# Head sums of branch A as rounded part and remainder

## What is computed

```
y = moveaxis(y, 0, 1)                                  # (B, T, heads, 64)
mean = jnp.mean(y, -1, keepdims=True)
var = jnp.mean(jnp.square(y - mean), -1, keepdims=True)
y = ((y - mean) * lax.rsqrt(var + RWKV_LN_EPS)).reshape(B, T, BW) * ln_g + ln_b
bonus = jnp.sum(r * k * r_k.reshape(H, N), -1, keepdims=True) * v
return y + bonus.reshape(B, T, BW)
```

## Time and profile before

| | |
|---|---|
| median of three runs | 1074.45 us |
| the profiled execution | 1073.86 us |
| its span | 1072.0 us |
| TensorE busy in the span | 1048.0 us, 98% |
| VectorE busy | 586.9 us, 55% |
| GpSimd busy | 371.9 us, 35% |
| ScalarE busy | 315.5 us, 29% |
| mean granted TensorE clock | 0.998 |

### The profile page before, as it was taken

One profiled execution on the slowest core, in us unless ns is written; L12 is line 12 of the kernel. 1 busy time (PEld: TensorE's weight loads), 2 busy tenths in 40 slices (PEclk: granted clock), 3 DMA queues, 4 the chain that ended last, 5 costly groups with the idle time before them and its releaser, 6 DMA issues.

```text
span 1072.0 us, 22528 instructions
## 1 busy us (share of the span) xinstructions
PE 1048.0 (98%) x9816; PEld 824.5 (77%) x9816; DVE 586.9 (55%) x988; ACT 315.5 (29%) x508; POOL 371.9 (35%) x343
## 2 busy tenths in 40 slices
PE   7999999999999999999999999999999999999997
PEld 5686787777777877877877777877877778878885
DVE  3768943874463522622623139458888587433553
ACT  5545112421503203213211133335444330002221
POOL 1431543321466222122231223353334249662000
PEclk9999999999999999999999999999999999999999
DMA  9700111211111110111111121111111137302221
GB/s 355 276 19 12 47 52 47 72 30 35 40 28 36 40 37 27 40 37 36 31 37 31 37 62 30 50 51 36 42 36 42 36 104 260 108 25 98 101 77 59
DMA packets 80130, 70.24 MB, mean 66 GB/s; under 512 B 4128, under 2 KB 68896, under 8 KB 80032
## 3 DMA queue, kind: packets, MB, share of 16 engines
q1 hardware_dynamic: 74560, 49.34, 14.8%
q10 hardware_dynamic: 5472, 19.47, 5.1%
HBM read 64.59 MB, written 4.19 MB: 64 GB/s over the span
## 4 chain that ended last, share of the span: by engine, by line
PE 88%; DVE 6%; DMA 2%; SPq 2%; ACT 1%; issue 1%; ACTq 0%; DVEq 0%
PE bank L609 55%; PE bank L663 8%; PE bank L1144 8%; PE bank L715 2%; PE bank L1099 1%; DVE slots L1744 1%; DMA slots<-in_x 1%; PE bank L941 1%; PE bank L937 1%; PE bank L820 1%; DMA slots<-in_w_mod 1%; PE bank L888 1%; SPq L437 1%; DVE slots L1824 1%; PE bank L914 1%; DVE slots L1728 1%
## 5 line engine op out<-in xcount | busy, mean ns | idle before, releaser
L609 PE MATMUL bank<-hn_hi,w_hi 128*128 128x512 f32 x880 | 357.0, 406 | 2.3 <-DVE slots L1886 1.7
L609 PE MATMUL bank<-hn_hi,w_lo 128*128 128x512 f32 x880 | 343.4, 390 | 0.0
L609 PE MATMUL bank<-hn_lo,w_hi 128*128 128x512 f32 x880 | 343.0, 390 | 0.0
L523 POOL CAST w_hi<-w_raw 128x512 fp32r<-128x512 f32 x110 | 86.3, 784 | 535.0 <-PE bank L609 535.0
L609 PEld LDWEIGHTS bank<-hn_hi,w_hi 128*128 128x128 f32 x880 | 165.1, 188 | 42.4 <-issue 4.3
L609 PEld LDWEIGHTS bank<-hn_hi,w_lo 128*128 128x128 f32 x880 | 165.2, 188 | 36.1
L609 PEld LDWEIGHTS bank<-hn_lo,w_hi 128*128 128x128 f32 x880 | 165.3, 188 | 33.8 <-issue 1.9
L525 POOL TENSOR_TENSOR w_lo<-w_raw,w_hi 128x512 fp32r<-128x512 f32 x110 | 154.2, 1402 | 8.8
L1276 ACT ACTIVATE stage<-bank 128x512 f32<-128x512 f32 x64 | 38.1, 599 | 247.5 <-PE bank L609 232.4
L1255 ACT ACTIVATE slots<-bank 128x512 f32<-128x512 f32 x42 | 24.8, 599 | 123.0 <-PE bank L609 122.9
L1884 DVE TENSOR_TENSOR stage<-stage,bank 128x512 f32<-128x512 f32 x48 | 33.0, 687 | 40.4 <-PE bank L663 39.0
(11 more groups left out here) (334 smaller groups left out, 1547.8 us busy)
## 6 DMA issues: line engine op xcount, KB each, us to landing
w_raw<-in_w_in SPq DMA_DIRECT2D x110, 256.0 KB, 2.8
slots<-in_w_mod SPq DMA_DIRECT2D x16, 512.0 KB, 11.4
slots<-in_x SPq DMA_DIRECT2D x8, 512.0 KB, 9.2
w_branch<-in_w_branch SPq DMA_DIRECT2D x32, 128.0 KB, 2.9
slots<-in_w_mod ACTq DMA_DIRECT2D x8, 512.0 KB, 4.9
slots<-in_w_out ACTq DMA_DIRECT2D x8, 512.0 KB, 6.2
xr<-in_x ACTq DMA_DIRECT2D x8, 512.0 KB, 3.6
out<-xr ACTq DMA_DIRECT2D x8, 512.0 KB, 2.6
```

The source lines that it names most:

```text
L523: nc.gpsimd.tensor_copy(w_hi[p][:, :, :], w_raw[p][:, :, :]).then_inc(s_pool_step, 1)
L609: last = mm(o, w[p][:, k4, :], h[:, k, n * HALF:(n + 1) * HALF], start=(p == 0 and k4 == 0 and q == 0), stop=(p == 1 and k4 == 3 and q == 2))
```

## The change

A fp32 product per bank becomes two products of rounded operands, one with the input's rounded part and one with its remainder, added up in the bank; the stationary operand is `ones_r`, the table of ones copied once into a rounded tile. ScalarE makes the rounded parts by a copy and VectorE the remainders by a subtraction, for the mean (rounded part in slots 14 and 15, remainder in slots 6 and 7), for the variance (the same slots again, the remainder in place of the squares) and for the bonus (rounded part in slots 0 and 1, remainder in place in slots 8 and 9). The bonus input (L2058) is made earlier, ahead of the forget gate. The scan (L2065) waits for the variance group, as it writes slots 14 and 15.

```diff
--- before.py
+++ after.py
@@ -200,6 +200,8 @@
         s_a_sa_ready = sem("a_sa_ready")
         s_a_gnew_done = sem("a_gnew_done")
         s_a_mean_done = sem("a_mean_done")
+        s_sum_hi_ready = sem("sum_hi_ready")
+        s_sum_lo_ready = sem("sum_lo_ready")
         s_a_rk_ready = sem("a_rk_ready")
         s_a_bonus_done = sem("a_bonus_done")
         s_a_bonus_read = sem("a_bonus_read")
@@ -277,6 +279,7 @@
         lru_w_at = -(-nc.sbuf_base // 32) * 32
         lru_w = sb("lru_w", [P, 4, P])
         small = sb("small", [P, 80])
+        ones_r = sb("ones_r", [P, P], F32R)
         banks = ctx.enter_context(nc.psum_tensor("bank", [P, 8, HALF], F32))
         bank = [banks[:, i, :] for i in range(8)]
 
@@ -406,6 +409,9 @@
 
         y_lo = {s0: nc.alloc_sbuf_tensor_at(f"y_lo{s0}", [P, 2, T], F32R, offset=slots_at + row * s0)
                 for s0 in sorted(set(Y_SLOT.values()))}
+        sum_hi = [over(f"sum_hi{j}", slots_at + row * (14 + j), F32R) for j in range(2)]
+        bonus_hi = [over(f"bonus_hi{j}", slots_at + row * j, F32R) for j in range(2)]
+        bonus_lo = [over(f"bonus_lo{j}", slots_at + row * (8 + j), F32R) for j in range(2)]
         w_branch_lo = [nc.alloc_sbuf_tensor_at(f"w_branch_lo{i}", [P, 2, P], F32R, offset=w_branch_at + 8 * P * i)
                        for i in range(2)]
         w_branch_hi = [nc.alloc_sbuf_tensor_at(f"w_branch_hi{i}", [P, 2, P], F32R, offset=lru_w_at + 8 * P * i)
@@ -811,6 +817,10 @@
                 project_part(1 + j)
             project_part(3)
 
+            def sums_of(o, hi, lo, n):
+                mm(o[:, :], ones_r[:, :], hi[:, n * HALF:(n + 1) * HALF], start=True, stop=False)
+                return mm(o[:, :], ones_r[:, :], lo[:, n * HALF:(n + 1) * HALF], start=False, stop=True)
+
             def head_sums(src, turn):
 
 
@@ -1030,21 +1040,25 @@
             project(4)
             pe.wait_ge(s_a_y_ready, 16)
             pe.wait_ge(s_a_g_ready, 32)
+            pe.wait_ge(s_sum_hi_ready, 1)
 
             for j in range(2):
                 for n in range(2):
-                    mm(bank[4 + 2 * j + n][:, :], blockones, slot(4 + j)[:, n * HALF:(n + 1) * HALF],
-                       start=True, stop=True).then_inc(s_a_mean_done, 1)
+                    if n == 0:
+                        pe.wait_ge(s_sum_lo_ready, j + 1)
+                    sums_of(bank[4 + 2 * j + n], sum_hi[j], y_lo[6][:, j], n).then_inc(s_a_mean_done, 1)
             project(1)
-            head_sums(6, 2)
+            for j in range(2):
+                pe.wait_ge(s_sum_lo_ready, j + 5)
+                for n in range(2):
+                    sums_of(bank[4 + 2 * j + n], sum_hi[j], y_lo[6][:, j], n).then_inc(s_head_sums, 1)
             project_part(0)
             project_part(1)
             for j in range(2):
-                pe.wait_ge(s_a_rk_ready, j + 1)
+                pe.wait_ge(s_sum_lo_ready, j + 3)
                 for n in range(2):
                     pe.wait_ge(s_roots, 8 + 2 * j + n + 1)
-                    mm(bank[4 + 2 * j + n][:, :], blockones, slot(8 + j)[:, n * HALF:(n + 1) * HALF],
-                       start=True, stop=True).then_inc(s_a_bonus_done, 1)
+                    sums_of(bank[4 + 2 * j + n], bonus_hi[j], bonus_lo[j], n).then_inc(s_a_bonus_done, 1)
             turn_tile(BI)
             project_part(2)
             project_part(3)
@@ -1454,6 +1468,15 @@
 
             act.wait_ge(s_a_y_ready, 16)
             act.wait_ge(s_a_g_ready, 32)
+            nc.scalar.activation(ones_r[:, :], blockones, ACT.Copy).then_inc(s_sum_hi_ready, 1)
+            after(s_sum_hi_ready)
+            for j in range(2):
+                nc.scalar.activation(sum_hi[j], slot(4 + j), ACT.Copy).then_inc(s_sum_hi_ready, 1)
+                after(s_sum_hi_ready)
+            for j in range(2):
+                act.wait_ge(s_a_rk_ready, j + 1)
+                nc.scalar.activation(bonus_hi[j], slot(8 + j), ACT.Copy).then_inc(s_sum_hi_ready, 1)
+                after(s_sum_hi_ready)
             evac(2)
             for j in range(2):
                 nc.scalar.activation(b_f[j], b_f_raw[j], ACT.Sigmoid).then_inc(s_b_f_sig, 1)
@@ -1467,7 +1490,10 @@
             evac(2)
             act.wait_ge(s_a_centred, 4)
             squares(4, 6)
-            act.wait_ge(s_a_rk_ready, 2)
+            for j in range(2):
+                act.wait_ge(s_squares, 4 + j + 1)
+                nc.scalar.activation(sum_hi[j], slot(6 + j), ACT.Copy).then_inc(s_sum_hi_ready, 1)
+                after(s_sum_hi_ready)
             evac(1)
             roots(6, 2, 1.0 / 64, "ln_eps")
             act.wait_ge(s_b_d_ready, 1)
@@ -2040,6 +2066,22 @@
 
 
             for j in range(2):
+                dve.wait_ge(s_sum_hi_ready, j + 2)
+                dve.wait_ge(s_br_done, 32)
+                nc.vector.tensor_tensor(y_lo[6][:, j], slot(4 + j), sum_hi[j].bitcast(F32), SUB)\
+                    .then_inc(s_sum_lo_ready, 1)
+                dve.wait_ge(s_sum_lo_ready, after(s_sum_lo_ready))
+            for j in range(2):
+                nc.vector.scalar_tensor_tensor(out=slot(8 + j), in0=slot(8 + j), scalar=pc("rk", j),
+                                               in1=slot(10 + j), op0=MUL, op1=MUL).then_inc(s_a_rk_ready, 1)
+                dve.wait_ge(s_a_rk_ready, after(s_a_rk_ready))
+            for j in range(2):
+                dve.wait_ge(s_sum_hi_ready, j + 4)
+                nc.vector.tensor_tensor(bonus_lo[j], slot(8 + j), bonus_hi[j].bitcast(F32), SUB)\
+                    .then_inc(s_sum_lo_ready, 1)
+                dve.wait_ge(s_sum_lo_ready, after(s_sum_lo_ready))
+
+            for j in range(2):
                 dve.wait_ge(s_b_f_sig, j + 1)
                 nc.vector.tensor_scalar(b_f[j], b_f[j], omlb[:, j:j + 1], lball[:, j:j + 1], MUL, ADD)\
                     .then_inc(s_vector_step, 1)
@@ -2055,10 +2097,12 @@
                                                    in1=y, op0=MUL, op1=ADD).then_inc(s_a_centred, 1)
                     dve.wait_ge(s_a_centred, after(s_a_centred))
             for j in range(2):
-                nc.vector.scalar_tensor_tensor(out=slot(8 + j), in0=slot(8 + j), scalar=pc("rk", j),
-                                               in1=slot(10 + j), op0=MUL, op1=MUL).then_inc(s_a_rk_ready, 1)
-                dve.wait_ge(s_a_rk_ready, after(s_a_rk_ready))
-
+                dve.wait_ge(s_sum_hi_ready, j + 6)
+                nc.vector.tensor_tensor(y_lo[6][:, j], slot(6 + j), sum_hi[j].bitcast(F32), SUB)\
+                    .then_inc(s_sum_lo_ready, 1)
+                dve.wait_ge(s_sum_lo_ready, after(s_sum_lo_ready))
+
+            dve.wait_ge(s_head_sums, 12)
             dve.wait_ge(s_reset128_landed, 16)
             for j in range(2):
                 dve.wait_ge(s_b_lnf, j + 1)
```

## The result

The changed kernel takes 1069.18 us (median of 4 runs, 1068.79 to 1069.56) against 1074.43 us for the kernel before on the same chip (4 runs). The ratio is 0.9953, with a 95% interval from 0.9936 to 0.9970. The forecast was 1069.6 us.

What follows compares the result with a forecast made beforehand. TensorE, busy in 98% of the span, was taken as the bound. The 4.83 us saved by Term 1, with all other terms at 0, came off the median of 1074.45 us: 1069.6 us, range 1068.9 to 1071.2.

Steps and rivals of the forecast that it cites:

- Term 1: Mean, variance and bonus groups on TensorE: 1.82 us each instead of 3.43, saving 4.83 us for three.
- The rival that rounded products don't run faster here: Products in the three groups stay at 0.43 us each, time as before, 1074.4 us; chance 0.05.
- Term 2: New ScalarE and VectorE work before the mean group, done at about 600 us, fits idle time; cost 0.
- Term 3: Between mean and variance group: second remainder ready at 644.9 to 646.9 us, 1.6 us or more left; cost 0.
- Term 4: Scan waits for variance group; turned tile BI out at 663.1, TensorE asks at 663.8 before BQ; stall 0.
- The rival of a stall at BQ: TensorE stalls 0.1 to 1.4 us before tile BQ's first half, about 1070.3 us; chance 0.17.
- Term 5: Branch A's output chain on VectorE moves some 6.5 us, last bonus bank read about 684, 3 us in hand; cost 0.
- given back later: Rival: branch A's delayed output chain pushes back branch B's loop; 1071.0 us if 4.4 us late; chance 0.03.
- The rival of the loop as the bound: Variance group, scan, exponents, exponential, evacuation, TensorE become the bound; at 22 us of loop, 1078.1 us; chance 0.02.

Runs made afterwards that it cites:

- work_only: Changed kernel with all new copies, subtractions and waits, but full fp32 products in the three groups again; 1074.07 us, 1.0000 of the kernel before.
- after_again: The changed kernel measured once more, no edit; 1069.17 us, 0.9952 of the kernel before.
- experiment 8: Changed kernel with both scans done twice, but free to start before the variance group (also called twice_free); 1070.10 us, 0.9962 of the kernel before.
- scan_twice: Changed kernel with both scans done twice, lengthening the chain behind the variance group; 1074.85 us, 1.0003 of the kernel before.
- scan_free: Changed kernel with the variance's rounded part in free rows of y_hi, so the scan doesn't wait; 1069.17 us, 0.9952 of the kernel before.
- hi_only: Changed kernel with the remainder's product left out of all three sums; 1067.45 us, 0.9941 of the kernel before.
- after: The changed kernel itself, as first measured and profiled; 1069.18 us, 0.9953 of the kernel before.
- twice_free: Changed kernel with both scans done twice, but free to start before the variance group; 1070.10 us, 0.9962 of the kernel before.
- b_group: Changed kernel with branch B's end group of head sums also split into rounded products, two merge pieces moved ahead; 1071.70 us, 0.9977 of the kernel before.

## Why the prediction was right

**Term 1, the products.** Right: 1.83 us a group at 0.23 us per product (forecast 1.82); by its pieces the three save 4.79 us and the whole stretch 4.82 (4.83). work_only and after_again, 1074.07 and 1069.17 us, put it at 4.9 us by medians. The rival that rounded products don't run faster here falls with it.

**Term 2, the new work ahead.** Right. ScalarE's copies and VectorE's four subtractions and two multiplications were done at 600.5 us (forecast 600), with 16.0 us of idling left. work_only shows it free.

**Term 3, between mean and variance group.** Right. The second remainder was ready at 645.7 us, inside 644.9 to 646.9; the variance group started at 649.17. That is over 3 us in hand, where the prediction had at least 1.6.

**Term 4, the moved wait.** Right in place and size, with the 0.64 us taken off by which the execution ran later: scan at 650.5 (650.4), last exponents at 660.1 (659.9), turned tile out at 663.3 (663.1), TensorE asking at 663.8 (663.8), 0.6 us in hand (0.7). Inside it two sizes were off and half cancelled, which is luck: the scans took 4.67 us, not 4.88, and there were two hold-ups of 1.5 us together (0.42 + 1.09), not one of 1.1. (The upper end of the exponents was also added up wrong: 658.7 + 0.61 + 1.26 is 660.6, not 660.8. With it the largest stall is about 0, not 0.3 us; the forecast doesn't use it.) The prediction left out that the Trainium skill's rule (SBUF — State Buffer, SBUF: two separate sides) is for GpSimd operations that read SBUF, as in experiment 8; both operations of the split read it. scan_twice shows that the slack is real and that nothing else absorbs a late chain; scan_free that there is no stall to remove; hi_only that it is gone when TensorE gets 0.9 us faster beside it and the scans meet one more split of the weights. The rival of a stall at BQ (0.1 to 1.4 us) did not happen.

**Term 5, the output chain.** Right. The last bonus bank was read at 684.7 us (684), before the evacuation that ended at 687.95. Nothing was given back later: behind the transposes the span is 0.4 us shorter, not longer.

**The sum.** 1069.6 forecast, 1069.18 measured. No step accounts for the 0.4 us; as shown above, it is of the size by which the median of the kernel before wanders from batch to batch. The rival of the loop as the bound was priced from 20.4 us of loop on; in after it took 12.9 us (651.0 to 663.9). With 4.3 us more, scan_twice was already no faster than the kernel before. By the working of that rival a loop of 17.2 us costs 17.2 - 13.5 = 3.7 us of stall, which gives 1073.3 us, and 1074.85 was measured: it left out what follows a wait, in the profiled execution 2.8 us at the lower clock.

## What to carry to other kernels

A full fp32 product with a constant table of ones costs about twice as much as two rounded ones (0.86 against 0.46 us here), so the split pays wherever the copies and subtractions fit into time that their engines idle and are ready before TensorE asks; look for that before making the edit, group by group. A group on TensorE is also the cover of its neighbours: where the engine that must make the copies is the one that TensorE waits for next, shortening the group costs more than it saves. When a wait moves, follow the whole loop that it closes back to TensorE and write down the slack in us; here, with 0.6 us in hand, the moved wait cost nothing, and a chain 4.3 us longer took back the whole gain.

## What the runs showed that I had not expected

- The price of one longer wait of TensorE is more than the wait: 3.6 us of idling was followed by 4 us at a granted clock of 0.50 and 4 at 0.84, and cost 2.8 us more (scan_twice). After waits of 0.5 us (twice_free) and 1.1 us (hi_only) the next windows stayed at 1.00.
- The waits view understates short waits of TensorE, as it counts from the modelled end of the product before: 2.7 us of waits in b_group cost 4.0 us from start to start.
- The scans and GpSimd's split hold each other up in both directions: 0.61 us became 2.47, and 2.29 became 3.26 (twice_free). In after the scans took 4.67 us for two, as GpSimd was between two splits for nearly all of that time (651.3 to 656.6 us).
